# A mixture-of-experts stage: the weights of four experts held in buffers of their own, their blocks set between streamed ones

## The reference, cut to what matters

```python
def _hier_moe(h, w_group, b_group, w_expert, b_expert, w1, w3, w2):
    g_prob = jax.nn.softmax((h @ w_group) + b_group, axis=-1)
    g_top_p, g_top = lax.top_k(g_prob, 1)
    e_logits = ...            # the 8 logits of the chosen group
    e_top_p, e_top = lax.top_k(jax.nn.softmax(e_logits, axis=-1), TOP_K)
    ...                       # rows sorted by expert, padded to whole blocks
    def expert_block(args):
        xe, e = args
        return (jax.nn.silu(xe @ w1[e]) * (xe @ w3[e])) @ w2[e]
    ...                       # summed into the rows with weight g_top_p * e_top_p
```

## Time and profile before

| | us |
|---|---|
| median of 3 runs | 4379.66 (4377.66 to 4379.9) |
| the profiled execution: its own time | 4363.92 |
| the profiled execution: its span | 4362.1 |
| PE matmul busy in the span | 3440.5 (79%) |
| DVE busy | 1591.8 (36%) |
| ACT busy | 811.0 (19%) |
| first load of expert weights to the last down product, layer one | 1040.91 to 1338.34 |
| first load of router data to the first load of expert weights, layer one | 969.07 to 1040.91 |

### The profile page before, as it was taken

The page is one execution under the profiler, slowest core; times in us unless marked ns, Lnnn a source line. Parts: engine busy times, 40 slices in busy tenths (PEclk is TensorE's granted clock), DMA queues, the critical chain, the costliest instruction groups (busy, mean ns, idle before and its releaser), DMA issues. The chain is left out here.

```text
span 4362.1 us, 75094 instructions
## 1 busy us (share of the span) xinstructions
PE 3440.5 (79%) x32104; PEld 2327.7 (53%) x32104; DVE 1591.8 (36%) x2752; ACT 811.0 (19%) x1591; POOL 331.4 (8%) x462
## 2 busy tenths in 40 slices
PE   0698599674774897699575774777998899999998
PEld 0565499563443665599463443244765764444444
DVE  3334455512113344555421114135545651124411
ACT  0221222120221111222121221002334310010000
POOL 0000122002111000221002111000003200000000
PEclk9999699896997998799787997888999999999999
DMA  3200000014993200000016993601001022222221
GB/s 145 71 32 13 22 5 5 2 56 175 398 396 117 83 30 22 2 5 5 21 42 238 395 400 128 217 15 40 30 10 50 1 68 87 77 68 77 68 60 46
DMA packets 190336, 405.55 MB, mean 93 GB/s; under 512 B 39981, under 2 KB 139693, under 8 KB 161693
## 3 DMA queue, kind: packets, MB, share of 16 engines
q1 hardware_dynamic: 170029, 354.56, 22.4%
q0 software_dynamic: 9776, 29.92, 2.1%
q10 hardware_dynamic: 10240, 16.79, 1.1%
HBM read 384.45 MB, written 37.99 MB: 97 GB/s over the span
## 5 line engine op out<-in xcount | busy, mean ns | idle before, releaser
L2881 PE MATMUL ps<-h_lat,wt 128*128 128x512 f32 x704 | 304.2, 595 | 5.9 <-ACT h_lat L2938 5.9
L1629 PE MATMUL ps<-e_w,e_xt 128*64 128x256 f32 x2048 | 248.2, 396 | 9.2 <-DMA e_w<-in_moe_w 5.4
L588 PE MATMUL ps<-h,win 128*128 128x264 f32 x960 | 232.6, 396 | 17.4 <-DVE pad L737 15.9
L1629 PEld LDWEIGHTS ps<-e_w,e_xt 128*64 128x64 f32 x2048 | 177.7, 145 | 112.0 <-issue 64.7
L2881 PEld LDWEIGHTS ps<-h_lat,wt 128*128 128x128 f32 x704 | 134.4, 191 | 175.7 <-issue 174.4
L588 PEld LDWEIGHTS ps<-h,win 128*128 128x128 f32 x960 | 180.3, 192 | 67.9 <-issue 39.3
L1648 PE MATMUL ps<-e_w,e_hid_t 128*64 128x512 f32 x512 | 158.5, 747 | 29.3 <-ACT e_hid_t L1676 29.3
L2838 PE MATMUL ps<-h_lat,wt 128*128 128x512 f32 x384 | 168.6, 597 | 8.2 <-DMA wt<-in_w_in 8.2
L1695 DVE TENSOR_TENSOR e_hid<-ps,e_silu 64x256 f32<-64x256 f32 x64 | 38.9, 608 | 330.1 <-ACT e_silu L1670 330.1
L2899 PE MATMUL ps<-ff_up,wt 128*128 128x512 f32 x352 | 152.2, 592 | 0.0
L1210 DVE COPY_PREDICATED inv<-level,ps 112x384 f32<-112x384 int32 x176 | 103.5, 588 | 80.6 <-PE ps L1106 71.8
(11 more groups left out here) (529 smaller groups left out, 6506.6 us busy)
## 6 DMA issues: line engine op xcount, KB each, us to landing
e_w<-in_moe_w SPq DMA_DIRECT2D x192, 1024.0 KB, 10.0
wmod<-in_w_mod SPq DMA_DIRECT2D x24, 1024.0 KB, 12.9
wt<-in_w_up SPq DMA_DIRECT2D x22, 1024.0 KB, 5.1
y_rows<-e_y ACTq DMA_DIRECT2D x128, 128.0 KB, 7.4
win<-in_w_in SPq DMA_DIRECT2D x10, 1536.0 KB, 6.4
wt<-in_w_in SPq DMA_DIRECT2D x12, 1024.0 KB, 7.6
wt<-in_w_down SPq DMA_DIRECT2D x16, 704.0 KB, 4.9
wout<-in_w_out SPq DMA_DIRECT2D x8, 1024.0 KB, 5.1
```

What stands on the lines that cost most here:

```text
L588: last = pe.matmul(ps[:, 7, 0:HT], lhsT=ring[(s + 1) % 2][:, i, o:o + P], rhs=k.h[:, i, h * HT:(h + 1) * HT], start=(i == 0), stop=(i == K ...
L1629: last = pe.matmul(ps[half, 2 + z, 0:EH], lhsT=xt[z][:, f, :], rhs=w[:, f, :], start=(f == 0), stop=(f == KD - 1))
L2881: last = pe.matmul(o, lhsT=w[:, i, m % 2 * P:(m % 2 + 1) * P], rhs=hl[:, i, :], start=(i == 0), stop=(i == KD - 1))
```

## The change

Four experts (`PRE`, numbers 0 to 3) get buffers `early` of their own, 12 MiB in all. ACT issues their 12 loads as the first thing of `route`'s first stage. Each of the four has one fixed block, whatever its number of rows; rows beyond 64 go to further blocks of the streamed kind. The loop of `experts` is peeled: 16 blocks are written out, one with early weights and then three streamed ones (`ring`), four times over, and the loop runs the rest of the streamed blocks in pairs. Within a block the order of work on each engine is kept. The semaphores start from 0, without the credits that stood in for buffers free at the start. DVE gets five operations at the head of the second routing stage (one is the memset that stood further down) and six where it had one, after the count.

```diff
-NBLK += NBLK % 2
+PRE = 4
+AHEAD = 3 * PRE
+DYN = NBLK - PRE + (NBLK - PRE) % 2
+NBLK = PRE + DYN + (PRE + DYN) % 2
...
         @block.scalar
         def _(act):
+            for n in range(PRE):
+                for dst, d in zip(early[n], expert_weights(a)):
+                    act.dma_start(dst[:, :, :], d[bass.ds(li * EXPERTS + n, 1), :, :, :].rearrange(
+                        "a p t n -> (a p) t n")).then_inc(early_in[n], 16)
             for j in range(NC1):
                 act.wait_ge(turned, j + 1)
...
+            chain(dve.tensor_scalar(later[:, :], iota[:, 0:EXPERTS], float(PRE), None, ALU.is_ge))
+            chain(dve.tensor_scalar(shift[:, :], later[:, :], float(SLOT), float(SLOT * (PRE - 1)), ALU.mult, ALU.add))
+            chain(dve.tensor_scalar(own_row[:, :], iota[:, 0:EXPERTS], float(SLOT), None, ALU.mult))
+            chain(dve.tensor_tensor(own_row[:, :], own_row[:, :], shift[:, :], ALU.subtract))
+            chain(dve.memset(ones32[:, :], 1.0))
...
-            chain(dve.tensor_tensor(t32[:, :, :], ps[0:TC, 0, 0:NC1 * EXPERTS].rearrange(
-                "p (j e) -> p j e", j=NC1), nb[:, None, :].to_broadcast([TC, NC1, EXPERTS]), ALU.add))
+            chain(dve.tensor_tensor(moved[:, :], own_row[:, :], nb[:, :], ALU.subtract))
+            chain(dve.tensor_tensor(nb[:, :], nb[:, :], shift[:, :], ALU.add))
+            chain(dve.scalar_tensor_tensor(moved[:, :], later[:, :], 0.0, moved[:, :], ALU.is_equal, ALU.mult))
+            ranks = ps[0:TC, 0, 0:NC1 * EXPERTS].rearrange("p (j e) -> p j e", j=NC1)
+            chain(dve.scalar_tensor_tensor(t32[:, :, :], ranks, float(SLOT),
+                                           moved[:, None, :].to_broadcast([TC, NC1, EXPERTS]), ALU.is_lt, ALU.mult))
+            chain(dve.tensor_tensor(t32[:, :, :], t32[:, :, :], ranks, ALU.add))
+            chain(dve.tensor_tensor(t32[:, :, :], t32[:, :, :],
+                                    nb[:, None, :].to_broadcast([TC, NC1, EXPERTS]), ALU.add))
...
+    first = []
+    for t in range(PRE):
+        first += [("early", t)] + [("ring", AHEAD // PRE * t + n) for n in range(AHEAD // PRE)]
+    S0 = len(first)
...
+            for n in range(AHEAD):
+                load(n % 2, owner[0:1, n:n + 1],
+                     spot(first.index(("ring", n - 2))) if n >= 2 else None)
             with turns(sp) as i:
-                for z in Z:
-                    e = sp.value_load(owner[0:1, bass.ds(2 * i + z, 1)], min_val=0, max_val=EXPERTS - 1)
...
+                for r in Z:
+                    load(r, owner[0:1, bass.ds(2 * i + (AHEAD + r), 1)], in_loop(i, r - 2))
...
+            for s, (kind, n) in enumerate(first):
+                z, c = spot(s)
+                nz, ncnt = spot(s + 1)
+                if kind == "early":
+                    one_block(z, c, (nz, ncnt), early[n], (early_in[n], 48), None, c > 0, ncnt > 0)
+                else:
+                    r, j = n % 2, n // 2
+                    one_block(z, c, (nz, ncnt), (w1[r], w3[r], w2[r]), (up_w[r], 32 * j + 32),
+                              (down_w[r], 16 * j + 16), c > 0, ncnt > 0)
             with turns(pe) as i:
```

More of the change, by code:

```diff
@@ L150, in _ @@
                 def _(sp):
-                    for s in sems:
+                    for s in sems + self.also:
                         sp.sem_clear(s)
@@ L1530, in _, with experts @@
             chain(dve.tensor_copy(pairs[:, :], ownf[:, 0:1]))
-def experts(k, a, li, ex, slots, owner, pairs):
+def experts(k, a, li, ex, slots, owner, turns_left, early, early_in):
     nc, ps = k.nc, k.ps
@@ L1586, in fetch, with load @@
-        def fetch(gp, z):
-            gp.indirect_dma_start(
-                out=x[z][:, :], out_offset=None, in_=k.h_rows[:, :],
-                in_offset=bass.IndirectOffsetOnAxis(ap=idx[z][:, 0:1].bitcast(U32), axis=0),
-                bounds_check=T - 1, oob_is_err=False).then_inc(x_in[z], 16)
+            def load(r, n, released):
+                e = sp.value_load(n, min_val=0, max_val=EXPERTS - 1)
+                row = li * EXPERTS + e
+                one = lambda d: d[bass.ds(row, 1), :, :, :].rearrange("a p t n -> (a p) t n")
+                if released is not None:
+                    z, c = released
+                    sp.wait_ge(up[z], c + 1)
+                sp.dma_start(w1[r][:, :, :], one(d1)).then_inc(up_w[r], 16)
+                sp.dma_start(w3[r][:, :, :], one(d3)).then_inc(up_w[r], 16)
+                if released is not None:
+                    sp.wait_ge(down[z], c + 1)
+                sp.dma_start(w2[r][:, :, :], one(d2)).then_inc(down_w[r], 16)
@@ new lines, in store @@
+            def store(z, c, rows):
+                act.wait_ge(y_kept[z], c + 1)
+                for q, half in enumerate((low, high)):
+                    act.dma_start(k.y_rows[rows, q * 512:(q + 1) * 512], y[z][half, :]).then_inc(y_out[z], 16)
+            keep_rows(0, 0, False)
+            for s, (kind, n) in enumerate(first):
+                z, c = spot(s)
+                nz, ncnt = spot(s + 1)
+                one_block(z, c, (nz, ncnt), c > 0, ncnt > 0)
+                if s:
+                    pz, pc = spot(s - 1)
+                    r0 = column(*first[s - 1]) * SLOT
+                    store(pz, pc, slice(r0, r0 + SLOT))
@@ new lines, in _ @@
+            pz, pc = spot(S0 - 1)
+            r0 = column(*first[S0 - 1]) * SLOT
+            store(pz, pc, slice(r0, r0 + SLOT))
+            n_turns = act.value_load(turns_left[0:1, 0:1], min_val=1, max_val=DYN // 2 - AHEAD // 2)
+            with act.Fori(0, n_turns) as i:
+                for r in Z:
+                    z, c = in_loop(i, r)
+                    one_block(z, c, in_loop(i, r + 1), True, True)
+                for r in Z:
+                    z, c = in_loop(i, r)
+                    store(z, c, bass.ds((2 * i + S0 + r) * SLOT, SLOT))
```

235 lines of the change are left out of this document (125 added, 110 removed).

## The result

| | before | changed |
|---|---|---|
| median of 13 runs each, us | 4382.54 | 4391.84 |
| lowest to highest, us | 4372.55 to 4393.51 | 4387.81 to 4398.37 |
| ratio of the medians, 95% interval | 1 | 1.0022 [1.0012, 1.0032] |
| profiled execution, us (span) | 4363.92 (4362.1) | 4388.28 (4386.5) |

The change makes the kernel 9.3 us slower, a little over the 0.2% that can be told from no change. Against the median of the three runs that the forecast was made from, the ratio gives 4389. I compare stretches that begin at an event of the same stage instead: the store of the empty list (`row_tok`, the first issue of the routing), and the first load of expert weights in SP's stream.

A forecast was written before the change was run, and what follows sets the result against it. Expert loop bound equally by the PE, ACT, DVE chain with its table load and by the DMA engines. A layer: -28.5 experts, +25 first routing, +1.4 second = -2.1 us; two layers -4.2, giving 4375.5 us, range 4342 to 4394.

The forecast's parts named there:

- narrower range of 4361 to 4391: Whole kernel: the main forecast's own range, with small loads landing at 991 to 1002 and loop blocks of 8.6 to 9.1 us.
- By 971 the small ones had a start of about 370: First routing stage: about 370 of SP's 1483 small packets through by 971, the other 1113 taking 22.9 us, to 994.
- landing term: First routing stage: SP's small transfers, one packet for one against 8 KB weight packets, land at 997; logits wait for them.
- The cold PE: First routing stage: after about 15 us of waiting PE runs all six logits groups at 1.2 GHz, 17.8 us.
- ACT's late copies of `h`, hidden by the landing: First routing stage: 12 issues delay ACT's copies some 6 us, to near 975; the wait for small transfers hides it.
- The second routing stage, +1.4 us: Second routing stage: added small operations cost 0.1 us before the exponential and 1.3 behind the count, between 1 and 2.5.
- The blocks written out: Expert stage, 16 peeled blocks: 7.35 us each from the second on, block 16's up product at 1172.2, 23 us gained.
- The loop at 8.8 us from block 18: Expert loop: transfers limit blocks to 8.8 us from block 18; last up product at 1301.3 in place of 1330.80.
- Four more semaphores, "nothing that could show": End of a stage: four more semaphores are cleared, forecast to cost nothing that could show.
- Rival 1: First routing stage: small transfers get through while weights run; 4356 us, or 4341 with no hold-up at all; chance 0.24.
- Rival 2: Expert loop: two clock dips a block make it 10.35 us, not 8.8; 22 us a layer, 4419 us; chance 0.11.
- Rival 3: Expert loop: transfers have room, blocks run at 8.4 us; 5 us more gained a layer, 4365 us; chance 0.05.

## Why the prediction was wrong, point by point

I forecast 4375.5 us, gain and price cancelling, and gave "slower" 0.20. The time, 4391.84, lies in the range of 4342 to 4394, near its upper end, and on the slower side of 0.2%. The mechanisms were the ones described and no rival took over; the sum was off in two terms that both erred the same way: the routing costs 29.0 and 29.3 us a layer and not 26.4, the expert stage gains 25.2 and 23.3 and not 28.5. Against a difference of two terms of some 28 us each, 3 to 5 us in each decide the sign. The narrower range of 4361 to 4391 was also added up unevenly: -7 to +6 us a layer around the sum of -2.1 is 4361 to 4387, and the two layers lie 5.9 and 8.1 us above the sum.

- **"By 971 the small ones had a start of about 370", so they land by 997.** This is the step that failed: the head start of the small transfers in the landing term. In the kernel before, SP's queue had indeed moved 341 packets by 971, 1.9 us behind its first issue, and I carried such a start over to a stage in which ACT issues weights at the same time. In the changed kernel it had moved none by 975, 2.2 us behind its first issue (972.84), and 43 by 976, when the weights had 75. From there 1440 stood in line: at the 48.6 a us that I had worked out they need 29.6 us, which from 976 is 1005.6, and the logits start at 1005.25. The one-for-one turns were right; that the time fits so well is partly luck, since the trace has 52 a us up to 1002 and a slow rest. Measured from the list's store the logits start 4.5 us later than forecast, and the copy of the logits moves by 28.7 us instead of 24.5, which I had rounded to 25. Why the small queue's first packets came so late stays open: ACT's first issue is only 0.15 us ahead of SP's, and from 974 to 975 the weights kept the engines busy only 37%. No run put SP's issues just ahead of ACT's.
- **The cold PE**: right. All six groups at granted clock 0.50, 17.6 us in all (forecast 17.8).
- **ACT's late copies of `h`, hidden by the landing**: right in the changed kernel (copies end at 991.8, logits wait until 1005.25), but I had them start 2.5 us too early: ACT's 12 issues take 8.5 us and not 6, 0.71 each. The kernel with the small loads first shows that cover gone: 13 us.
- **The second routing stage, +1.4 us**: +0.2 before the exponential and +1.2 from it to the reading of the slot table, as forecast. From there to the first load it is 1.0 us less, which I had missed; SP no longer reads the number of turns before it. Copy of the logits to the first load: +0.4.
- **The blocks written out**: right to half a microsecond. 7.35 us each, block 16's up product 130.8 us behind the first load, 131.3 forecast. In it two small misses cancel: the first up product starts 11.3 us behind the load and not 10.4, and the first block, no longer 10.6 us, takes 9.1.
- **The loop at 8.8 us from block 18**: the second mis-sized term. It is 8.9 us, from block 17 on, though I had given it two more blocks at 7.35. I read that as a stream with nothing in hand at the end of the written-out part, where the DMA share was 0.98 already; that was not tried by itself. The 15 steps take 133.8 us instead of 129.1. The stage gains 25.2 and 23.3 us and not 28.5.
- **Four more semaphores, "nothing that could show"**: from the last copy of DVE to the first gather of the combine it is 0.22 and 0.26 us more in the two layers. Small, but not nothing; that the semaphores are the reason was not tried.
- **Rival 1, small packets not held up one for one**: wrong by the counts (116 and 116), and by the landing. By the rule of the Trainium skill that I weighed there (DMA: Bandwidth & Descriptors, Queues, rings and completion order: up to 64 descriptors before an engine turns to the other queue) the landing would have been near 987 us, 18 us behind the list's store; the logits' wait ended 32.4 us behind it. The measurement decides: with full engines, the turns of SP's and ACT's queues are single packets of the trace. (The burst in the run with 4 KB packets fell where the engines were not full of weights.)
- **Rival 2, the clock dips in the loop**: it did not take over: granted clock 0.99 over the loop of layer one, with one product at a lower clock (1302.69), although PE waits in nearly every block. **Rival 3, room in the transfers**: against it stand the runs with a third less to load and with the table load out of the loop.

What would have warned of the error: writing down the first issue of each engine in the order that the stage gives them. ACT has nothing to wait for, while SP first waits for `blank_set`; so a start taken from a stage in which SP was alone had no ground.

## What to carry to other kernels

Idle transfer time can be used, but not in the stretch where a chain waits for small transfers: SP's and ACT's queues share the engines by packets, and a load in packets of under 512 B beside one in packets of 8 KB got 5% of the engines. Put a prefetch where it is through before the chain needs the next transfer, on an engine that would be idle; here this choice alone was worth 56 us. It hung on the weights being through 9 us before the last scatter; a longer prefetch in that place was not tried. And when a term gains as much as another loses, do each to the microsecond or widen the chance of both signs.

## What the runs showed that I had not expected

- The issues themselves took longer beside queued transfers. SP's last small load took 4.38 us to issue beside the weights, 0.35 before; ACT's twelve took 8.5 us, and 24 of half the size 21.3 us (0.71 and 0.89 each; a store in the loop 0.48). An engine that issues is not free to compute.
- The table load, 1.28 us in each turn, and the clock dips behind it cost the kernel before 2 us a layer, though in the earlier trace rows they make one block 2.7 us longer than the other: the transfers took the rest back.
- The packets of GpSimd's scatters stood still beside the weights on SP's queue. Its issues kept their 1.28 us steps, so the engine looks unharmed, but none of the 96 packets of three scatters moved while the weights ran, and 92 came in the us in which they ended. The same kernel on another chip shows it too: 91 packets from 1029 to 1030, none before. That is not one for one, as between SP's and ACT's queues, and why is open. Whoever reads only the issues takes this for no collision.
- In layer one of the changed kernel the product behind a wait kept its 3.67 us for waits up to 1.7 us, yet the granted clock fell behind 1.92 us of idle time in the earlier trace rows and behind 1.99 us at 1302.69. What decides it is open.
